# A chunked RWKV-7 recurrence on one core: unpadded factors, head pairs on 64 rows each, and inversion levels that carry only the 64 columns they change

## The reference

```python
def step(state, inp):
    r_t, w_t, k_t, v_t, a_t, b_t = inp
    sa = jnp.einsum('bhvk,bhk->bhv', state, a_t)
    state = state * w_t[:, :, None, :] + sa[..., None] * b_t[:, :, None, :] + v_t[..., None] * k_t[:, :, None, :]
    return state, jnp.einsum('bhvk,bhk->bhv', state, r_t)
```

## Time and profile before

| | us |
|---|---|
| median of 3 runs | 4860.31 (4856.0 to 4862.63) |
| profiled execution | 4860.21 |
| its span | 4858.4 |
| granted TensorE clock, mean | 0.98 of full |

### The profile page before, as it was taken

How to read it: one execution, slowest core, us unless ns; L and a number is a source line. 1 busy time by engine, 2 the same in 40 slices (tenths; PEclk the granted TensorE clock), 3 DMA queues, 4 the chain that set the end, 5 groups by cost and what they waited for, 6 DMA issues and landing times. The chain is left out here.

```text
span 4858.4 us, 64349 instructions
## 1 busy us (share of the span) xinstructions
PE 4624.5 (95%) x24100; PEld 3699.9 (76%) x24100; DVE 2462.1 (51%) x4115; ACT 1539.1 (32%) x2178; POOL 315.0 (6%) x169
## 2 busy tenths in 40 slices
PE   6997999999999999897899999979999999999999
PEld 3454888888888888643799989938888888888887
DVE  5764875553245555520655555427945542444444
ACT  1252333333222222202333444313333332222222
POOL 0001340000000000003000000003410000000000
PEclk9999999999999999899899999989999999999999
DMA  6302345656566666234000000022455665555553
GB/s 239 126 1 78 104 142 186 216 197 212 172 234 227 226 221 240 91 122 162 31 19 23 18 19 18 1 76 80 148 169 202 211 208 173 194 195 187 185 195 137
DMA packets 248144, 690.90 MB, mean 142 GB/s; under 512 B 12921, under 2 KB 78713, under 8 KB 239905
## 3 DMA queue, kind: packets, MB, share of 16 engines
q1 hardware_dynamic: 240544, 654.99, 39.6%
q0 software_dynamic: 7424, 33.56, 1.9%
HBM read 533.27 MB, written 155.22 MB: 142 GB/s over the span
## 5 line engine op out<-in xcount | busy, mean ns | idle before, releaser
L1321 DVE TENSOR_TENSOR pe_lo<-pe_raw,pe_hi 128x2048 fp32r<-128x2048 f32 x222 | 509.0, 2293 | 1266.7 <-ACT pe_hi L1101 1266.7
L796 PE MATMUL bank<-pe_hh,pe_hi 128*128 128x512 f32 x2304 | 913.7, 397 | 51.0 <-POOL pe_lo L1199 49.7
L798 PE MATMUL bank<-pe_hh,pe_lo 128*128 128x512 f32 x2304 | 900.1, 391 | 0.0
L797 PE MATMUL bank<-pe_hl,pe_hi 128*128 128x512 f32 x2304 | 899.7, 390 | 0.0
L796 PE MATMUL bank<-pe_ah,pe_hi 128*128 128x512 f32 x2048 | 796.7, 389 | 0.0
L797 PE MATMUL bank<-pe_al,pe_hi 128*128 128x512 f32 x2048 | 796.7, 389 | 0.0
L798 PE MATMUL bank<-pe_ah,pe_lo 128*128 128x512 f32 x2048 | 796.7, 389 | 0.0
L1101 ACT ACTIVATE pe_hi<-pe_raw 128x2048 fp32r<-128x2048 f32 x272 | 520.4, 1913 | 588.8 <-PE bank L798 580.1
L796 PEld LDWEIGHTS bank<-pe_hh,pe_hi 128*128 128x128 f32 x2304 | 433.8, 188 | 140.5 <-POOL pe_lo L1199 51.6
L798 PEld LDWEIGHTS bank<-pe_hh,pe_lo 128*128 128x128 f32 x2304 | 433.6, 188 | 91.4
L797 PEld LDWEIGHTS bank<-pe_hl,pe_hi 128*128 128x128 f32 x2304 | 434.2, 188 | 85.7
(11 more groups left out here) (277 smaller groups left out, 5581.7 us busy)
## 6 DMA issues: line engine op xcount, KB each, us to landing
pe_raw<-in_stream SPq DMA_DIRECT2D x272, 1024.0 KB, 5.6
acts<-h SPq DMA_DIRECT2D x128, 512.0 KB, 7.6
gates<-pe_stage SPq DMA_DIRECT2D x32, 2048.0 KB, 7.4
pe_w<-gates SPq DMA_DIRECT2D x32, 2048.0 KB, 10.3
h<-acts SPq DMA_DIRECT2D x128, 512.0 KB, 4.0
ada_ring<-in_ada_w SPq DMA_DIRECT2D x32, 768.0 KB, 7.4
at_ada_ring<-in_ada_w POOLq DMA_DIRECT2D x16, 1024.0 KB, 7.4
rwkv_proj<-rp_out POOLq DMA_DIRECT2D x64, 256.0 KB, 2.7
```

Of the source, the lines that this page charges most:

```text
L796: nc.tensor.matmul(out, left[0], right[0], start=start, stop=False)
L797: nc.tensor.matmul(out, left[0], right[1], start=False, stop=False)
L798: return nc.tensor.matmul(out, left[1], right[0], start=False, stop=stop)
L1321: nc.vector.tensor_tensor(lo[:, side], raw[:, side], hi[:, side].bitcast(F32), ALU.subtract).then_inc(low, 1)
```

## The change

- A and R have no padding: `[P, 2, 2, T]`, one instruction on 128 partitions for each. POOL no longer clears them, and DVE signals 4 factors for a chunk rather than 6.
- A new `products(kind, z, ...)` replaces `four` and `two` in the products stage. It forms, for one direction, eight products of 64 contracted rows: four blocks, the two heads after each other, each head from its own 64 partitions and into its own PSUM bank. `BANKS` gives the ten calls four pairs of banks in rotation.
- A level of the inversion works on one direction with eight units, not on four groups. P and Q have 64 moving columns, picked from T by a strided view (`changed`); DVE writes them back with a strided view of T and of the mask. In the last level Q has 64 weight columns and 64 moving columns and lands in 64 partitions, and DVE copies it without a mask.
- The group norm is split into `center`, which stands after the products, and `rescale` after level 1; `gated_sum`, the transposes of y (now in bank 6) and ACT's `affine` are in or after level 2; ACT's `deviation` follows level 1. The parts of `front` follow whole levels.
- In the scan A times S and R times S are one product each.

```diff
-        A = sb("A", [P, 2, 2, TC, 2, P])
-        R = sb("R", [P, 2, 2, TC, 2, P])
+        A = sb("A", [P, 2, 2, T])
+        R = sb("R", [P, 2, 2, T])
...
-        FRONT_AT = ((1, 1), (1, 3), (2, 1), (2, 3), (3, 3), (4, 3), (5, 1), (5, 3))
-        ACT_FRONT_AT = ((1, 3), (2, 3), (3, 1), (3, 3))
+        FRONT_AFTER = {1: (0,), 2: (2, 3), 3: (4, 1), 4: (5,), 5: (6, 7)}
+        ACT_FRONT_AFTER = {2: (0,), 4: (3, 1), 5: (2,)}
...
+        def changed(m, z, lv):
+
+            return m.rearrange("p u (k two w) -> p u k two w", two=2, w=1 << lv)[:, :, :, z, :]
...
+        KINDS = ("N", "NT", 0, 1, 2)
+        BANKS = {(kind, z): 2 * ((5 * z + i) % 4) for z in range(2) for i, kind in enumerate(KINDS)}
...
                         for dst, d, by in ((A, dA, kk[:, :]), (R, dR, r)):
-                            for h in range(2):
-                                rows = slice(h * HD, (h + 1) * HD)
-                                nc.vector.tensor_tensor(
...
+                            nc.vector.tensor_tensor(dst[:, side], d[:, :, :], twice(by), ALU.mult).then_inc(factors, 1)
...
+                    for lv in range(1, NLEV + 1):
+                        for z in range(2):
+                            dve.wait_ge(q_done, PER * c + pair(lv, z))
                             dve.sem_inc(waited, 1)
+                            if lv < NLEV:
+                                mask = masks[:, z, lv:lv + 1, :].to_broadcast([P, 8, P])
+                                nc.vector.copy_predicated(changed(groups_of(Tm, z), z, lv), changed(mask, z, lv),
+                                                          compact(bank8(2 + z), lv)).then_inc(inv_out, 1)
+                            else:
+                                nc.vector.tensor_copy(groups_of(TT, z)[HEADS[z], :, HEADS[1 - z]], bank8(2 + z)[HEADS[z]]
+                                                      ).then_inc(inv_out, 1)
...
+                def products(kind, z, left, right, side, sem_, free=None):
+
+                    for b in range(TC):
+                        at = slice(b * P, (b + 1) * P)
+                        for h in range(2):
+                            if b == 0 and free is not None:
+                                pe.wait_ge(free[0], free[1] + h)
+                            last = nc.tensor.matmul(K.ps[BANKS[kind, z] + h][:, at], left[HEADS[h], side, z, at],
+                                                    right[HEADS[h], side, z, at], start=True, stop=True)
+                            if b == TC - 1:
+                                last.then_inc(sem_, 1)
...
+                    products("N", 0, A, B, side, n_done)
+                    products("NT", 0, B, A, side, nt_done, (tok_out, 5 * c + 1))
+                    products(0, 0, C, A, side, masked_done, (tok_out, 5 * c + 3))
+                    pe.wait_ge(tok_out, 5 * c + 5)
+                    products(1, 0, B, R, side, masked_done)
+                    products(2, 0, C, R, side, masked_done, (prod_out, made + 1))
+                    products("N", 1, A, B, side, n_done, (nt_out, 4 * c + 1))
+                    products("NT", 1, B, A, side, nt_done, (prod_out, made + 3))
+                    products(0, 1, C, A, side, masked_done, (prod_out, made + 5))
+                    products(1, 1, B, R, side, masked_done, (prod_out, made + 7))
+                    products(2, 1, C, R, side, masked_done, (prod_out, made + 9))
...
+                    def double_q(lv, z):
+                        pe.wait_ge(p_out, PER * c + pair(lv, z))
+                        pe.wait_ge(tt_out, TURNS * c + turn(lv, z, 1))
+                        t_of = lambda u: TT[:, 2 * z + u // 4, u % 4, :]
+                        p_of = lambda u: Pb[:, z, u, :]
+                        if lv < NLEV:
+                            eight(z, lambda u: K.ps[2 + z][:, u * HD:(u + 1) * HD], t_of, p_of, q_done)
+                        else:
+                            eight(z, lambda u: K.ps[2 + z][HEADS[z], u * HD:(u + 1) * HD], p_of,
+                                  lambda u: t_of(u)[:, HEADS[1 - z]], q_done)
 
                     for lv in range(1, NLEV + 1):
                         double_p(lv, 0)
                         double_p(lv, 1)
+                        if lv == 2 and not first:
+                            transpose_y(c - 1)
                         double_q(lv, 0)
+                        double_q(lv, 1)
...
-                            nc.tensor.matmul(K.ps[z][:, 0:P], A[:, side, z, blk[z], 0, :], S[:, b % 2, z],
-                                             start=True, stop=False)
+                            nc.tensor.matmul(K.ps[z][:, 0:P], over(A, z), S[:, b % 2, z], start=True, stop=False)
...
-                            nc.tensor.matmul(K.ps[z][:, 0:P], A[:, side, z, blk[z], 1, :], S[:, b % 2, z],
-                                             start=False, stop=True).then_inc(rhs_done, 1)
```

More of the change, by code:

```diff
@@ L1888, in body @@
[L1888 to L1897, removed]
+                    for z in range(2):
+                        for h in range(2):
+                            g4 = 2 * z + h
+                            dve.wait_ge(ident_ready, 4 * c + g4 + 1)
+                            dve.wait_ge(n_done, 4 * c + g4 + 1)
+                            dve.sem_inc(waited, 1)
+                            nc.vector.copy_predicated(Tm[:, g4], bc4(masks[:, z, 0, :]), bank4(BANKS["N", z] + h)
+                                                      ).then_inc(prod_out, 1)
+                        for i in range(3):
+                            for h in range(2):
+                                dve.wait_ge(masked_done, 12 * c + 6 * z + 2 * i + h + 1)
+                                dve.sem_inc(waited, 1)
+                                nc.vector.copy_predicated(MT[:, i, 2 * z + h], bc4(tri[:, 2 * z + (i > 0), :]),
+                                                          bank4(BANKS[i, z] + h)).then_inc(prod_out, 1)
@@ new lines, in body @@
+                    if not first:
+                        center(c - 1)
+                    for lv in range(1, NLEV + 1):
+                        for z in range(2):
+                            dve.wait_ge(q_done, PER * c + pair(lv, z))
+                            dve.sem_inc(waited, 1)
+                            if lv < NLEV:
[5 more added lines that the diff above has]
+                                                      ).then_inc(inv_out, 1)
+                        if lv == 1 and not first:
+                            rescale(c - 1)
+                        if lv == 2 and not first:
+                            gated_sum(c - 1, 1 - side)
+                        if not last:
+                            for part in FRONT_AFTER.get(lv, ()):
+                                front(part, c + 1, 1 - side)
@@ L1922, in body @@
                     round_up(NSTEP)
-                for part in range(len(FRONT_AT)):
+                for part in range(8):
                     front(part, 0, 0)
@@ L1987, in body @@
                             nc.scalar.activation(U[:, z], K.ps[2 + z][:, 0:P], ACT.Copy).then_inc(u_out, 1)
[L1989 removed]
+                for part in range(4):
                     front(part, 0, 0)
@@ L2079, in double_q, with eight @@
-                    def double_q(lv, g4):
-                        q = group(lv, g4)
-                        pe.wait_ge(p_out, 4 * NLEV * c + q)
-                        pe.wait_ge(tt_out, INV * c + q)
-                        if q > 2:
-                            pe.wait_ge(inv_out, INV * c + q - 2)
-                        t_of = lambda u: TT[:, g4, u, :]
-                        p_of = lambda u: Pb[:, g4 % 2, u, :]
-                        left, right = (t_of, p_of) if lv < NLEV else (p_of, t_of)
-                        four(2 + g4 % 2, left, right, q_done)
+                    def eight(z, out, left, right, sem_):
+                        for u in range(8):
+                            last = nc.tensor.matmul(out(u), left(u), right(u), start=True, stop=True)
+                        last.then_inc(sem_, 1)
```

182 lines of the change are left out of this document (76 added, 106 removed).

## The result

The changed kernel takes 4752.93 us (median of 4 runs, 4749.6 to 4757.0) against 4861.33 before (median of 4 runs): a ratio of 0.9779, 95% interval 0.9763 to 0.9796, 108 us less. The forecast was 4762, the range 4740 to 4806. Measured once more later, the same kernel gave 4753.24. The profiled execution of the changed kernel has a span of 4749.8 us.

What follows compares the result with a forecast made beforehand. PE was taken to bound the kernel, busy 95% of the span. Per chunk products -5.9, inversion -4.7, pause +1.5, switches +0.7, scan -3.55 make -12.0; eight chunks -96, with the start -98: 4762 us, range 4740 to 4806.

Steps and rivals of the forecast that it cites:

- products: Products stage of each chunk: PE halves with two heads at a time, DVE's copies set 15.4 us against 21.3, -5.9.
- inversion, full clock: Six levels of the inversion, without stalls: 54.6 us a chunk against 59.3, -4.7.
- pause: PE idle 3.6 us between products and inversion; the clock then falls to 1.2 GHz, costing 1.5 us a chunk.
- switches of the array: Four changes a chunk between 128 by 128, 64-row and 64-column use, 0.17 us idle each: +0.7 us a chunk.
- scan: Scan of each chunk: two products fewer per step and direction, 32 records at 0.111 us, -3.55 us.
- start: Before chunk 0 DVE's four factor instructions become two: 2.4 us saved, once.
- halved columns save PE nothing: Inversion levels: 80 records at 0.111 us, 8.9 us a level before and after, since 128 weight columns set the pace.
- halved load in the last level: Last level's Q loads 64 weight columns: 1.8 us saved a chunk, bounds nothing and 32 x 0.056.
- steps of 1.46: Products stage: calls 0.9 us long would come every 1.46 us, DVE's time for each pair of banks.
- Pairs that don't overlap: Rival, products stage: two heads don't run together at 128 columns; -7.1 us a chunk, 4801 us; chance 0.13.
- a clock that is low from within the products stage: Rival: short PE pauses between calls keep the clock low; -5.3 us a chunk, 4815 us; chance 0.12.
- rival of a low clock in the inversion: Rival: half the inversion at 1.2 GHz costs 27 us a chunk, slower than before, 5030 us; chance 0.04.

Runs made afterwards that it cites:

- e5: The changed kernel with 128 moving columns again in P of all levels and Q of levels 1 to 5: 4745.88 us.
- e10: The changed kernel with 128 moving columns again in P and Q, repeated on the same chip as a rerun of the changed kernel: 4740.19 us.
- e12: The e8 kernel with 128 instead of 64 weight columns in seven of eight units of the last level's Q: 4790.32 us.
- e1: The changed kernel with ten throwaway identity products filling PE's pause before the inversion: 4734.59 us.
- e4: The changed kernel with A times S and R times S of the scan each made twice: 4779.98 us.
- e6: The changed kernel with 128 instead of 64 weight columns in seven of eight units of the last level's Q: 4806.34 us.
- e11: The e6 kernel, 128 weight columns in the last level's Q, measured again: 4815.11 us.
- e8: The e2 kernel with level 1's transposes of T, direction 0, moved ahead of P of direction 0: 4711.98 us.
- e3: The changed kernel with a products call's loops swapped, four blocks of head 0, then four of head 1: 4763.32 us.
- e2: The changed kernel where level 1's P and Q wait only for the copies that empty their banks, not all 16: 4722.38 us.
- e9: The changed kernel as it is, measured again on one chip beside e10: 4753.24 us.

## Why the prediction was right

**Where it stood by its own steps.** The forecast was 9 us too high. Per chunk, by a middle chunk's trace:

| step | forecast | measured |
|---|---|---|
| products | -5.9 | -7.2 (21.3 to 14.15) |
| inversion, full clock | -4.7 | -4.8 (59.31 to 54.47) |
| pause | +1.5 | +1.8 (14.5 in eight chunks) |
| switches of the array | +0.7 | none seen beyond the above |
| scan | -3.55 | -3.6 (24.77 to 21.19) |
| start | -2.4 once | -2.6 (PE's wait for the last factor of chunk 0, 13.4 to 10.8) |

The measured steps add up to -13.8 a chunk, -110 in all. Chunk 7 gave 2.3 less in its inversion, which makes the 108 us by which the recurrence shrank. The miss of 9 is what is left of errors of both signs: products and switches were forecast too dear, the pause too cheap, and the last inversion's gain too large. The start's 2.6 us lies ahead of the recurrence, which yet begins only 1.1 us earlier, since the stages ahead differ by more than that between traces.

**Inversion.** The count of 80 records per level at 0.111 held, and so did "halved columns save PE nothing" (e5, e10) and the halved load in the last level: 0.056 a record in its rows, +1.55 when undone (e12). The levels have no stall. That most of the 3.3 us of stalls before came from `front` is argued; no run moved its parts alone. Chunk 7, which has no `front` to do and no sums at level 3, bears it out: by the prediction's sum it had 1.0 us of stalls before, and its inversion shrank by 2.5 us only. Busy time by stretch, the kernel before, then e1 (chunk 7's inversion at the full clock):

```profile
3098.44:3153.75 55.31, 54.38 (x481) 53.88 (x481) 17.55 (x24) 26.05 (x48) 0.00 (x0) 1.00 0.01 1
...
2979.33:3032.15 52.82, 51.92 (x486) 51.62 (x485) 14.44 (x21) 21.16 (x39) 0.00 (x0) 1.00 0.01 1
```

The forecast took eight equal chunks. One copy came close to making a stall: DVE's copy into T takes 1.33 us in level 1, where the run of changed columns is two elements long, against 0.70 from level 2 on. That I had at 0.73; the limit named in the prediction was about 1.3. Timeline of chunk 6, level 1, then level 2:

```profile
2911.72 1.33 DVE L1915 COPY_PREDICATED rm_T<-rm_masks,bank 128x512 f32<-128x512 uint32 x1 [4.49 <-PE bank L2085]
...
2913.20 1.95 PE L2085 MATMUL bank<-rm_T,x 128*128 128x64 f32 x16
...
2920.97 0.70 DVE L1915 COPY_PREDICATED rm_T<-rm_masks,bank 128x512 f32<-128x512 uint32 x1 [2.52 <-PE bank L2085]
```

The first copy ends at 2913.05, and P of level 2 starts right behind it, with no idle time on its row.

**Products.** That two heads run at a time, and that DVE then sets the pace, held. The term that was mis-sized is the copy: I multiplied 16 by the mean duration 0.728, but copies that follow each other start 0.61 us apart. The row of six in 3.76 us shows it: five steps of 0.61 and one duration. From the first start to the last end the sixteen take 10.5 us, 0.45 of it a wait for PE's third call, not 11.65. The same error made the pause: 3.6 us forecast, 2.5 measured. The sign "steps of 1.46" did not come: the ten calls followed each other every 0.89 us, since copies of 0.61 freed their banks in time. The trace of before had shown the step, in three copies of its products stage that take two steps of 0.61 and one duration:

```profile
2445.10 1.94 DVE L1883 COPY_PREDICATED rm_MT<-rm_tri,bank 128x512 f32<-128x512 uint32 x3
```

I used starts for PE and durations for DVE.

**Pause.** The clock fell at the place that was forecast, in seven of eight chunks, and e1 shows the price alone. The pause was shorter than forecast and the price higher, since two drops lasted 6.8 us.

**Switches.** The 0.17 us stands before the first call on 64 rows (before the last level's Q the same 0.17 is put down to ACT), but the sum of 0.7 was not confirmed: the level and stage lengths are explained without it. The Trainium skill's sentence in TensorEngine Tiling (Array Packing), Key Properties, that a change of mode drains the engine, agrees with those 0.17 us; no run here prices it apart.

**Scan.** 32 records fewer at 0.111, back again when added (e4). The state was ready in time, as the 0.1 us of slack had it.

**Rivals.** Pairs that don't overlap, and a clock that is low from within the products stage, did not come. The rival of a low clock in the inversion did not come either: no drop there was longer than 6.8 us. But e6, e11 and e12 show a low clock over a whole stage, in the scan, after an edit that this rival did not name.

## What to carry to other kernels

Before a stage is cut on one engine, list what the next engine then sets, and what PE's new pause does to the clock: here a pause of 2.5 us cost more than filling it with useless work. Split a wait for "all copies" by what each instruction overwrites; that and moving ready work ahead took 35 us more out of the recurrence (e8). Time chained instructions by start to start on every engine, not by their duration.

## What the hardware showed that was not expected

- After products on 64 rows, pauses of PE of 1.2 us (e3) and 2.5 us were followed by 3.4 to 10.2 us at 1.2 GHz, where the kernel before had some 1.1 us at the same place in every chunk and no drop. With pauses of 0.7 us or none (e2, e8) no inversion opened with one. Whether the 64-row products or the length of the pause makes the difference between 1.1 and 1.2 us was not tried apart.
- Loading 128 rather than 64 weight columns in 28 of the last level's 32 records was followed in some chunks by 41 to 58 us at 1.2 GHz (e6, e11, e12).
- With 64 moving columns instead of 128 in the level after a pause, the drops were longer or more frequent (e9 against e10, two traces of each kind), though each record costs the same.
- Records on different row halves overlap out of the order of the program, but not far: with eight records of one half in a row, only the last three ran beside the first three of the other, 1.11 us a call against 0.89 side by side (e3).
- A predicated copy with a strided target costs 1.33 us for runs of two elements and 0.70 for runs of four and more, at 512 elements in both.
